# Two experts' slots filled at a time, 22 leading weight pieces, and narrower gathers in a streaming mixture-of-experts step

## The chip, the cores and the metric

The kernel runs on one core of a Trainium2 chip. The metric is the device time of one execution in microseconds (us): here the median of three runs. The program's engines are PE (TensorE), DVE (VectorE), ACT (ScalarE), POOL (GpSimd) and SP (SyncE, which here only issues loads). The core's 16 DMA engines are shared by all queues.

## What is computed

One layer of a hybrid encoder for 256 prompt rows and 32 sample rows (288 rows, 2048 wide): a combined input projection, stick-breaking attention, a gated linear recurrence, two gated projections and an output projection. Then a mixture of experts, which is the part that the change touches:

```python
def hmoe(h, wg, bg, ws, bs, wu, wd):
    hf = h.reshape(-1, d)
    g_logits = (hf @ wg) + bg
    _, g_idx = lax.top_k(g_logits, 1)                 # one of 4 groups
    ...
    e_val, e_idx = lax.top_k(sub_sel, TOP_K)          # two of its 4 experts
    e_w = jax.nn.softmax(e_val, axis=-1) * p_g
    combine = jnp.sum(one_hot(g_idx * 4 + e_idx, 16) * e_w[..., None], axis=1)
    for e in range(N_EXPERTS):                        # 16
        gate, up = jnp.split(hf @ wu[e], 2, axis=-1)  # wu[e]: 2048 x 1024
        out = out + combine[:, e:e+1] * ((silu(gate) * up) @ wd[e])   # wd[e]: 512 x 2048
```

Inputs and weights are float32. After it comes a final RMSNorm with a gain.

## The kernel before

**The stages.** Projections and attention run first and fill about 1080 us; their weights pass through four `ring` buffers. The output projection (`wo`, 16 column tiles) follows, with the router's logits. The experts come last.

**The experts' weights.** They are a stream of 192 pieces of 1 MB each (`STREAM`): 12 of each expert, 8 of `expert_w_up` ("up", two of the 16 row blocks k each) and 4 of `expert_w_down` ("down"). Pieces are numbered 0 to 191 here. Piece n goes to buffer `SLOT[n]` of `raw`. 16 buffers are permanent (`PERM`), and `ONCE = 4` more are used once, so `LEAD = 20` pieces can be loaded before any has been used. SP issues the pieces in order, each behind a wait: pieces 0 to 16 behind the progress of `wo`; piece 17 behind the first gather (`xs_in`) and the writes that it reads (`x1_out`), since its buffer lies where the table and the rows of before were; and from piece 20 on piece n waits until PE has used up the piece that was in its buffer (`eh_done`). From there on SP is 16 pieces ahead of PE at most.

**The rows.** An expert works on up to 64 rows. Per group of four experts, POOL gathers the group's rows (up to `CAP = 96`) from a table in DRAM into `xs`, in one indirect DMA of 128 rows of 7,680 bytes and one of 512 bytes each. PE then multiplies the transposed rows by one-hot matrices `R` ("spread"), one product for each of the 16 row blocks k, 256 columns wide (4 experts of 64 slots); two of them fill a PSUM bank. ACT and DVE empty the banks into `hgs`, multiplied by the norm's gain. Expert 0 can use its first piece when the first blocks are in `hgs`.

**The order of work** of PE, ACT and DVE around the pieces is written out by hand in half pieces t (piece n is t = 2n and 2n + 1). Tables say at which t something is slipped in: `SPREAD_AT` the spreads, `FIRST_ROWS` and `ROWS_AT` the transposes of `R` into `RT` and `es`, `META_AT` the next group's slots, `RESIDUAL_AT` four products that put the residual rows `xs` into the output banks `out4` (after which POOL may gather the next group into `xs`), `ADD_AT` the products that add an expert's output. `DOWN_AT[e]` is the t of expert e's first down piece; `DOWN_AT[0]` is 20 and `DOWN_AT[1]` is 44. `keep_warm(count)` issues that many products whose result nobody reads, while PE has nothing else to do.

Of the kernel before, what the change touches and what calls it, by code (L numbers as in the profile page):

```python
# [14 lines left out]
F32 = mybir.dt.float32  # L15
# [7 lines left out]
P = 128  # L23
# [27 lines left out]
PERM, ONCE = 16, 4  # L51
# [23 lines left out]
SLOT = [*range(13), *range(PERM, LEAD), *range(13, PERM)] + [n % PERM for n in range(PIECES - LEAD)]  # L75
# [43 lines left out]
NCONST, NCONST2 = 21, 13  # L119

# [33 lines left out]
def build(nc, x_prompt, x_sample, cache_k, cache_v, state_conv, state_lru, norm1_g, w_in, conv_w,  # L154
# [128 lines left out]
    lgT = sb("lgT", [40, T])  # L283
    best = sb("best", [TB, 5, 5 * FT, 4])
# [7 lines left out]
    hgs = sb("hgs", [P, 2, KT, EPG, ES])  # L292
    at_hgs1 = here[0] - 2 * 8192
# [33 lines left out]
    xs = sb("xs", [P, D])  # L327
    at_yo = here[0]
    yo = sb("yo", [CAP, D])
    gain = sb("gain", [P, D])  # L330
# [4 lines left out]
    here[0] = at_hgs1  # L335
    raw += [sb(f"raw{s}", [P, 2048]) for s in range(PERM + 2, LEAD)]
    assert here[0] <= at_o
    here[0] = at_prow
# [22 lines left out]
    up_v = expert_w_up[0].rearrange("e (p k) n -> p e k n", k=KT)  # L361
# [11 lines left out]
    with ExitStack() as ctx:  # L373
# [10 lines left out]
        trio = [bank[0:2], bank[2:4], bank[4:6]]  # L384

        x_in = [sem(f"x_in{f}") for f in range(FT)]
        par_in, rw_in, gain_in, gup_in = sem("par_in"), sem("rw_in"), sem("gain_in"), sem("gup_in")
# [58 lines left out]
        def spread_bank(q, c):  # L446

            return trio[q % 3][c] if q < SPREAD else work
# [15 lines left out]
        def _(sp):  # L464
# [12 lines left out]
            sp.dma_start(gup[:, :], norm2_g[0].rearrange("(p k) -> p k", k=KT)).then_inc(gup_in, 16)  # L477
# [53 lines left out]
            for dst, src in ((wr[:, :, 0:4], router_group_w[0].rearrange("(k p) g -> p k g", p=P)),  # L531
# [4 lines left out]
                sp.dma_start(dst, src).then_inc(rw_in, 16)  # L536
            gated_loads(T_PA, COL["ga"], w_pa_v)

            def fetch(slot, e, s, by_half=False):

                dst = raw[slot][:, :]
                if s < PU:
                    src = up_v[:, e, 2 * s:2 * s + 2, :]
                    dst = dst.rearrange("p (a k n) -> p a k n", a=1, k=2)
# [19 lines left out]
            for n, (e, s) in enumerate(STREAM):  # L564
# [6 lines left out]
                elif n == 14:  # L571
                    sp.wait_ge(half_done, 2 * T_END)
                elif n == 17:
                    sp.wait_ge(x1_out, 16 * len(X1_PARTS) + 16)
                    sp.wait_ge(token_ps, 2)
                    sp.wait_ge(xs_in, 16)
                elif n >= LEAD:
                    sp.wait_ge(eh_done, 2 * BEFORE[n] + 2)
                fetch(SLOT[n], ds(e, 1), s, e == NE - 1)
                if n == GAIN_AT:  # L580
                    sp.wait_ge(eh_done, 2 * SLOT.index(GAIN_SLOT) + 2)
                    sp.dma_start(gain[:, :], final_norm_g.rearrange("(a n) -> a n", a=1).partition_broadcast(P))\
# [23 lines left out]
        def _(pool):  # L606
# [98 lines left out]
            for g in range(NG):  # L705
                if g + 1 < NG:
                    pool.wait_ge(token_ready, g + 2)
                    pool.wait_ge(outB, SPREAD * (g + 1))
# [20 lines left out]
        def _(a):  # L729
# [247 lines left out]

            def drain_spread(q):

                a.wait_ge(spreadA_ps, q + 1)  # L980
                for c in range(2):
                    k = 4 * (q % SPREAD) + c
                    ins = a.activation(hgs[:, q // SPREAD % 2, k, :, :].rearrange("p e s -> p (e s)"),
                                       spread_bank(q, 0)[:, 256 * c:256 * (c + 1)], ACT.Copy, scale=gup[:, k:k + 1])
# [58 lines left out]
            a.wait_ge(gup_in, 16)  # L1043
            for q in range(2):
                drain_spread(q)
            for t in range(HALF_N):
# [16 lines left out]
                if t == FIRST_ROWS:  # L1063
                    rows(0, bank[2])
# [3 lines left out]
                for q, at in enumerate(SPREAD_AT):  # L1068
                    if t == at[0]:
# [14 lines left out]
            with a.If(n > CAP):  # L1084
                def again(v, first, width):

                    with a.Fori(0, NG) as g:
                        with a.Fori(0, width) as w:
# [5 lines left out]
                            for k in range(KT):  # L1094
                                a.wait_ge(ovhg_ps, KT * it + k + 1)
                                a.activation(hgs[:, 0, k, :, :].rearrange("p e s -> p (e s)"),
                                             bank[4 + k % 4][:, 0:EPG * ES], ACT.Copy, scale=gup[:, k:k + 1])\
# [29 lines left out]
        def _(pe):  # L1127
            pe.wait_ge(consts2, NCONST2)
            pe.wait_ge(par_in, 16 * 9)
# [289 lines left out]
            def spread(dst, k):  # L1419

                return pe.matmul(dst.rearrange("p (e s) -> p e s", e=EPG), xs[0:CAP, k::KT], R[:, :, 0, :].bitcast(F32),
# [713 lines left out]
```

## Time and profile before

| | us |
|---|---|
| median of three runs (1686.56 to 1687.59) | 1687.1 |
| the profiled execution's own time | 1686.14 |
| its span, first to last instruction | 1684.3 |
| PE busy in it | 1610.3 |
| DVE busy | 720.2 |
| ACT busy | 639.7 |
| POOL busy | 139.1 |

The profile is of one execution. Its times count from the first instruction; 1.8 us of the execution's own time lie outside of the span. Matmuls are pipelined, so that a row with several of them ends later than the next begins; the start of the next row says more. A DMA's "us to landing" is from the issue to the last part's completion.

### The profile page before, as it was taken

Reading aid. Unit: us, or ns where it says so; the run is one execution under the profiler, and the core shown is the slowest. Engines: PE = TensorE matmul, PEld = TensorE weight load, DVE = VectorE, ACT = ScalarE, POOL = GpSimd, SP = SyncE. Lnnn points to the kernel's source line nnn. Section 1 sums busy time; section 2 is a strip of 40 time slices with the busy share of each in tenths; the row PEclk is TensorE's granted clock in tenths of the full one; section 3 lists DMA queues with packets and bytes.
Section 4 is the critical chain, followed back from the end, with each engine's and each line's share of the span. In section 5 each row is a group of like instructions: output and inputs, shape, how many; then the busy total and the mean of one; then the engine's idle time right before and its main releaser. Section 6 shows DMA issues by size and latency. Waiting matters only on the chain. (4 is left out here: it accounts for less than half of the span.)

```text
span 1684.3 us, 27482 instructions
## 1 busy us (share of the span) xinstructions
PE 1610.3 (96%) x10714; PEld 1295.7 (77%) x10714; DVE 720.2 (43%) x1072; ACT 639.7 (38%) x1078; POOL 139.1 (8%) x189
## 2 busy tenths in 40 slices
PE   5999999999999999999999999999999999989885
PEld 4999999999999999999999999999734334323221
DVE  5888886443445455455454444544310201101101
ACT  6666665333344444444443333544211211111202
POOL 1644441000000000000000000000000000000000
PEclk9999999999999999999999999999999999999998
DMA  8465556566656546546478567795899999999995
GB/s 215 129 165 159 152 160 177 150 172 177 189 145 190 146 139 189 151 133 187 86 202 217 150 168 188 207 298 180 301 359 422 421 421 421 421 421 421 422 421 233
DMA packets 404519, 400.28 MB, mean 238 GB/s; under 512 B 19504, under 2 KB 377248, under 8 KB 379392
## 3 DMA queue, kind: packets, MB, share of 16 engines
q1 hardware_dynamic: 391456, 383.31, 69.2%
q0 software_dynamic: 2560, 11.21, 2.1%
q10 hardware_dynamic: 10432, 4.79, 1.1%
q8 instruction: 47, 0.77, 0.2%
q14 instruction: 24, 0.20, 0.0%
HBM read 389.77 MB, written 13.43 MB: 239 GB/s over the span
## 5 line engine op out<-in xcount | busy, mean ns | idle before, releaser
L1164 PE MATMUL bank<-hH,wH 128*128 128x288 f32 x1792 | 536.1, 299 | 6.2 <-ACTq L799 2.7
L1615 DVE TENSOR_TENSOR wL<-ring,wH 128x1024 fp32r<-128x1024 f32 x320 | 387.9, 1230 | 353.7 <-ACT wH L736 346.1
L736 ACT ACTIVATE wH<-ring 128x1024 fp32r<-128x1024 f32 x320 | 335.6, 1058 | 517.3 <-PE bank L1166 446.8
L1165 PE MATMUL bank<-hL,wH 128*128 128x288 f32 x1792 | 528.9, 295 | 0.0
L1166 PE MATMUL bank<-hH,wL 128*128 128x288 f32 x1792 | 528.5, 295 | 0.0
L1164 PEld LDWEIGHTS bank<-hH,wH 128*128 128x128 f32 x1792 | 337.3, 188 | 13.5 <-issue 7.0
L1165 PEld LDWEIGHTS bank<-hL,wH 128*128 128x128 f32 x1792 | 337.4, 188 | 0.3
L1166 PEld LDWEIGHTS bank<-hH,wL 128*128 128x128 f32 x1792 | 337.2, 188 | 0.0
L1396 PE MATMUL bank<-raw,hgs 128*64 128x512 f32 x1024 | 242.7, 600 | 18.9 <-DMA raw<-in_expert_w_up 15.3
L1396 PEld LDWEIGHTS bank<-raw,hgs 128*64 128x64 f32 x1024 | 66.6, 136 | 162.2 <-issue 110.5
L1164 PE MATMUL bank<-oH,wH 128*128 128x288 f32 x512 | 150.7, 294 | 0.5 <-DVE oL L1712 0.5
L1165 PE MATMUL bank<-oL,wH 128*128 128x288 f32 x512 | 151.0, 295 | 0.0
L1166 PE MATMUL bank<-oH,wL 128*128 128x288 f32 x512 | 150.9, 295 | 0.0
L1396 PE MATMUL bank<-raw,actT 128*64 128x512 f32 x512 | 124.7, 601 | 8.3 <-DMA raw<-in_expert_w_down 7.8
L1984 DVE SCALAR_TENSOR_TENSOR silu<-bank,es,silu 64x512 f32<-64x512 f32 x16 | 12.1, 757 | 265.7 <-ACT silu L1020 265.7
L1164 PEld LDWEIGHTS bank<-oH,wH 128*128 128x128 f32 x512 | 96.3, 188 | 1.0 <-DVE oL L1712 0.7
L1165 PEld LDWEIGHTS bank<-oL,wH 128*128 128x128 f32 x512 | 96.3, 188 | 0.0
L1166 PEld LDWEIGHTS bank<-oH,wL 128*128 128x128 f32 x512 | 96.2, 188 | 0.0
L1396 PEld LDWEIGHTS bank<-raw,actT 128*64 128x64 f32 x512 | 32.9, 136 | 78.3 <-issue 56.8
L1020 ACT ACTIVATE silu<-bank,es 64x512 f32<-64x512 f32 x16 | 10.9, 681 | 198.7 <-PE bank L1396 198.6
L1350 PE MATMUL bank<-hH,wH 128*128 128x288 f32 x256 | 76.4, 299 | 0.0
L1351 PE MATMUL bank<-hL,wH 128*128 128x288 f32 x256 | 75.5, 295 | 0.0
(312 smaller groups left out, 1538.4 us busy)
## 6 DMA issues: line engine op xcount, KB each, us to landing
raw<-in_expert_w_up SPq DMA_DIRECT2D x128, 1024.0 KB, 26.0
ring<-in_w_in SPq DMA_DIRECT2D x112, 1024.0 KB, 6.3
raw<-in_expert_w_down SPq DMA_DIRECT2D x64, 1024.0 KB, 26.5
ring<-in_w_pb SPq DMA_DIRECT2D x16, 1024.0 KB, 9.1
ring<-in_w_pa SPq DMA_DIRECT2D x16, 1024.0 KB, 9.1
ring<-in_w_o SPq DMA_DIRECT2D x16, 1024.0 KB, 6.1
cK<-in_cache_k SPq DMA_DIRECT2D x16, 256.0 KB, 2.8
cV<-in_cache_v SPq DMA_DIRECT2D x16, 256.0 KB, 3.2
```

The source lines that it names most:

```text
L736: a.activation(wH[2 * (slot % 2) + half][:, :, :], ring[slot][:, 8 * half:8 * half + 8, :], ACT.Copy).then_inc(hi_ready, 1)
L1020: a.activation(silu[ES:P, :], upb[0:ES, :], ACT.Silu, scale=es[0:ES, e // EPG % 2, e % EPG, 4:5]).then_inc(silu_ready, 1)
L1164: pe.matmul(dst, hi, rH[:, k, :], start=(k == 0), stop=False)
L1165: pe.matmul(dst, hi, rL[:, k, :], start=False, stop=False)
L1166: ins = pe.matmul(dst, lo, rH[:, k, :], start=False, stop=(k == KT - 1))
L1350: pe.matmul(dst, hi, hH[:, k, :], start=(k == 0), stop=False, skip_group_check=True)
L1351: pe.matmul(dst, hi, hL[:, k, :], start=False, stop=False, skip_group_check=True)
L1396: ins = pe.matmul(dst[c * ES:(c + 1) * ES, :], w, raw[slot][:, 1024 * half + 512 * c:1024 * half + 512 * (c + 1)], start=first, stop=last)
L1615: v.tensor_tensor(lo[:, :, :], ring[slot][:, 8 * half:8 * half + 8, :], hi[:, :, :].bitcast(F32), ALU.subtract).then_inc(lo_ready, 1)
L1984: v.scalar_tensor_tensor(silu[ES:P, :], upb[ES:P, :], es[ES:P, e // EPG % 2, e % EPG, e % EPG:e % EPG + 1], silu[ES:P, :], ALU.mult, ALU.m ...
```

## The change

The numbering of pieces and of t stays, the order of `STREAM` too. What differs:

- **Two experts at a time.** `hgs` is laid out by group, pair of experts, k. For group 0 the spread is done for experts 0 and 1 first (products of 128 columns, four to a bank, `pair_step`, two banks ahead of the first piece and one each ahead of pieces 2 and 4), and for experts 2 and 3 between the halves of pieces 15 to 18. The other groups keep products of 256 columns. DVE empties the first bank of a step and ACT the second.
- **22 leading pieces.** `ONCE` is 6. The buffers used once lie partly in the space of `hgs`' other pairs. Piece 13 now waits for the end of `wo` (it did not). Pieces 14 to 17 follow without a wait, piece 18 behind the logits (`lg_ps`), and it is piece 19 that waits for the gather. From piece 22 on a piece waits for `eh_done`.
- **Later group work.** `ASSIGN_AT`, `META_AT`, `ROWS_AT` and `RESIDUAL_AT` count from the group's second expert, 24 half pieces later (the residual 18 later). The residual products no longer start the banks: expert 0's `add_rows` does.
- **96-row transfers.** The gathers and the final gain's broadcast fill 96 partitions in place of 128.
- **Layout of the up weights.** The 2048 input rows are assigned to partitions in blocks of 256 (two neighbouring rows a partition), so an up piece is 1 MB in one run of DRAM, where it was 128 runs of 8 KB, 64 KB apart. `gup` follows, in runs of 8 bytes (1,024) where it was 64 bytes (128), and its landing is among those that PE's first instruction waits for. The rows' columns are now read two apart for a product's weights, where it was 16 apart.
- `keep_warm(6)` after the first group's token product becomes `keep_warm(14)`.

```diff
-PERM, ONCE = 16, 4
+PERM, ONCE = 16, 6
-SLOT = [*range(13), *range(PERM, LEAD), *range(13, PERM)] + [n % PERM for n in range(PIECES - LEAD)]
+SLOT = [*range(13), PERM + 2, PERM, PERM + 1, *range(PERM + 3, LEAD), *range(13, PERM)] + [n % PERM for n in range(PIECES - LEAD)]
...
-ASSIGN_AT = [DOWN_AT[EPG * g] for g in range(NG - 1)]
-META_AT = [DOWN_AT[EPG * g] + 2 for g in range(NG - 1)]
-ROWS_AT = [DOWN_AT[EPG * g] + 6 for g in range(NG - 1)]
-RESIDUAL_AT = [DOWN_AT[EPG * g] + 10 for g in range(NG)]
-FIRST_ROWS = 8
-SPREAD_AT = [(None, None)] * 2 + [(2, 2), (4, 4)]
+ASSIGN_AT = [DOWN_AT[EPG * g + 1] for g in range(NG - 1)]
+META_AT = [DOWN_AT[EPG * g + 1] + 2 for g in range(NG - 1)]
+ROWS_AT = [DOWN_AT[EPG * g + 1] + 6 for g in range(NG - 1)]
+RESIDUAL_AT = [DOWN_AT[EPG * g + 1] + 4 for g in range(NG)]
+FIRST_ROWS = 12
+SPREAD_AT = [(None, None), (4, 8)] + [(DOWN_AT[0] + 11 + 4 * r, DOWN_AT[0] + 13 + 4 * r) for r in range(2)]
...
-    up_v = expert_w_up[0].rearrange("e (p k) n -> p e k n", k=KT)
+    up_v = expert_w_up[0].rearrange("e (s p k) n -> p e s k n", p=P, k=2)
...
-            sp.dma_start(gup[:, :], norm2_g[0].rearrange("(p k) -> p k", k=KT)).then_inc(gup_in, 16)
+            sp.dma_start(gup[:, :].rearrange("p (s k) -> p s k", k=2),
+                         norm2_g[0].rearrange("(s p k) -> p s k", p=P, k=2)).then_inc(par_in, 16)
...
-                elif n == 14:
+                elif n == 13:
                     sp.wait_ge(half_done, 2 * T_END)
-                elif n == 17:
+                elif n == 18:
+                    sp.wait_ge(lg_ps, 1)
+                elif n == 19:
                     sp.wait_ge(x1_out, 16 * len(X1_PARTS) + 16)
                     sp.wait_ge(token_ps, 2)
                     sp.wait_ge(xs_in, 16)
...
-                                            bass.IndirectOffsetOnAxis(ap=idx[:, column, 2:3], axis=0),
+                                            bass.IndirectOffsetOnAxis(ap=idx[0:CAP, column, 2:3], axis=0),
...
-                return pe.matmul(dst.rearrange("p (e s) -> p e s", e=EPG), xs[0:CAP, k::KT], R[:, :, 0, :].bitcast(F32),
+                c = 2 * P * (k // 2) + k % 2
+                return pe.matmul(dst.rearrange("p (e s) -> p e s", e=count), xs[:, c:c + 2 * P - 1:2],
+                                 R[:, first:first + count, 0, :].bitcast(F32),
                                  start=True, stop=True, skip_group_check=True)
...
-            keep_warm(6)
+            keep_warm(14)
...
-            for q in range(2):
-                spread_step(q, 0)
-                spread_step(q, 1)
+            pair_step(0, 0)
+            pair_step(0, 1)
```

**PE from the wait for the gather to piece 4.** `hH` rows are keep-warm products, `R,xs` rows spreads, `raw,hgs` rows up pieces (four products each), `ident,R` rows the transposes into `RT`. Before:

```order
L1320 MATMUL bank<-hH 128x288 x20
L1421 MATMUL bank<-R,xs 128x256 [waits R_ready,xs_in,last_ready]
L1421 MATMUL bank<-R,xs 128x256 x7
L1396 MATMUL bank<-raw_136,hgs 64x512 [waits raw_in0,outA,routed]
L1396 MATMUL bank<-raw_136,hgs 64x512 x3
L1421 MATMUL bank<-R,xs 128x256 [waits outB]
L1421 MATMUL bank<-R,xs 128x256 x3
L1396 MATMUL bank<-raw_137,hgs 64x512 [waits raw_in1]
L1396 MATMUL bank<-raw_137,hgs 64x512 x3
L1421 MATMUL bank<-R,xs 128x256 [waits outA]
```

After:

```order
L1337 MATMUL bank<-hH 128x288 x20
L1439 MATMUL bank<-R,xs 128x128 [waits R_ready,xs_in]
L1439 MATMUL bank<-R,xs 128x128 x7
L1413 MATMUL bank<-raw_136,hgs 64x512 [waits raw_in0,outB,routed]
L1413 MATMUL bank<-raw_136,hgs 64x512 x3
L1413 MATMUL bank<-raw_137,hgs 64x512 [waits raw_in1,outB]
L1413 MATMUL bank<-raw_137,hgs 64x512 x3
L1439 MATMUL bank<-R,xs 128x128 [waits outA]
L1439 MATMUL bank<-R,xs 128x128 x3
L1413 MATMUL bank<-raw_138,hgs 64x512 [waits raw_in2]
```

The eight spreads ahead of piece 0 are half as wide and cover all that pieces 0 to 3 need.

**SP from piece 12 to the piece behind the gather and the first ones behind `eh_done`.** Before (pieces 12 to 20):

```order
L552 DMA raw_183<-in_expert_w_up 128x2048 [waits half_done]
L552 DMA raw_187<-in_expert_w_down 128x2048
L552 DMA raw_188<-in_expert_w_up 128x2048 [waits half_done]
L552 DMA raw_189<-in_expert_w_up 128x2048
L552 DMA raw_190<-in_expert_w_down 128x2048
L552 DMA raw_160<-in_expert_w_up 128x2048 [waits xs_in,token_ps,x1_out]
L552 DMA raw_161<-in_expert_w_up 128x2048
L552 DMA raw_162<-in_expert_w_down 128x2048
L552 DMA raw_136<-in_expert_w_up 128x2048 [waits eh_done]
```

After (pieces 12 to 22):

```order
L556 DMA raw_183<-in_expert_w_up 128x2048 [waits half_done]
L556 DMA raw_189<-in_expert_w_down 128x2048 [waits half_done]
L556 DMA raw_187<-in_expert_w_up 128x2048
L556 DMA raw_188<-in_expert_w_up 128x2048
L556 DMA raw_190<-in_expert_w_down 128x2048
L556 DMA raw_191<-in_expert_w_up 128x2048
L556 DMA raw_192<-in_expert_w_up 128x2048 [waits lg_ps]
L556 DMA raw_160<-in_expert_w_down 128x2048 [waits xs_in,token_ps,x1_out]
L556 DMA raw_161<-in_expert_w_up 128x2048
L556 DMA raw_162<-in_expert_w_up 128x2048
L556 DMA raw_136<-in_expert_w_down 128x2048 [waits eh_done]
```

Piece 13 has moved behind the end of `wo`, and two more pieces stand ahead of the wait for the gather.

## Rows read from the trace of the kernel before

**Rows 1.** Page, part 2: the span in 40 slices of 42 us.

```profile
DMA  8465556566656546546478567795899999999995
GB/s 215 129 165 159 152 160 177 150 172 177 189 145 190 146 139 189 151 133 187 86 202 217 150 168 188 207 298 180 301 359 422 421 421 421 421 421 421 422 421 233
```

**Rows 2.** Stretches: length, engines' busy time (rows), PE clock, DMA share, GB/s.

```profile
1199.00:1204.00 5.00, 4.27 (x23) 4.27 (x24) 2.05 (x14) 0.00 (x0) 0.88 (x2) 0.66 0.71 226
1207.00:1214.00 7.00, 7.00 (x31) 3.86 (x29) 1.74 (x3) 1.68 (x4) 0.00 (x0) 1.00 1.01 427
1248.00:1256.00 8.00, 8.00 (x37) 2.64 (x38) 0.00 (x0) 0.50 (x1) 2.09 (x2) 1.00 0.58 183
1262.00:1600.00 338.00, 319.39 (x1432) 114.78 (x1430) 47.16 (x91) 56.73 (x109) 9.71 (x10) 1.00 1.01 421
```

**Rows 3.** Timeline of SP's queue: start, length with waits between, issues.

```profile
1187.76 1.07 SPq L552 DMA_DIRECT2D raw<-in_expert_w_up  x2
1188.88 0.66 SPq L552 DMA_DIRECT2D raw<-in_expert_w_down  x1
1204.57 0.80 SPq L552 DMA_DIRECT2D raw<-in_expert_w_up  x2
...
1239.91 14.12 SPq L552 DMA_DIRECT2D raw<-in_expert_w_up  x2
1255.41 0.33 SPq L552 DMA_DIRECT2D raw<-in_expert_w_down  x1
```

**Rows 4.** Timeline of PE, 1199 to 1249 us: start, length, instructions, idle before.

```profile
1199.73 0.68 PE L1405 MATMUL bank<-meta,G 96*96 96x12 f32 x6 [1.32 <-DVEq L1948]
1200.26 4.43 PE L1320 MATMUL bank<-hH 128*128 128x288 f32 x20
1204.53 3.81 PE L1421 MATMUL bank<-R,xs 96*128 96x256 f32 x16
1208.27 1.94 PE L1396 MATMUL bank<-raw,hgs 128*64 128x512 f32 x8
1210.14 2.15 PE L1421 MATMUL bank<-R,xs 96*128 96x256 f32 x8
1212.21 1.94 PE L1396 MATMUL bank<-raw,hgs 128*64 128x512 f32 x8
...
1219.74 0.55 PE L1411 MATMUL bank<-ident,R 96*128 96x96 f32 x4
1220.13 0.98 PE L1415 MATMUL bank<-ms,R 96*128 96x5 f32 x8
1221.04 7.09 PE L1396 MATMUL bank<-raw,hgs 128*64 128x512 f32 x32
1229.76 1.94 PE L1396 MATMUL bank<-raw,hgs 128*64 128x512 f32 x8 [1.63 <-DVE silu L1984]
...
1244.68 3.67 PE L1446 MATMUL bank<-xs,ident 96*96 96x512 f32 x8
1248.28 1.94 PE L1396 MATMUL bank<-raw,hgs 128*64 128x512 f32 x8
```

**Rows 5.** DMA issues at 1198, 1358, 1253.7 and 1255.4 us: us to landing.

```profile
xs<-x_rows,idx POOLq DMA_INDIRECT x1, 6.1
...
xs<-x_rows,idx POOLq DMA_INDIRECT x1, 10.0
...
raw<-in_expert_w_up SPq DMA_DIRECT2D x1, 1024.0 KB, 4.9
...
raw<-in_expert_w_down SPq DMA_DIRECT2D x1, 1024.0 KB, 7.2
```

**Rows 6.** Groups by line and shape, 1190 to 1262 us: busy us, mean ns.

```profile
L1421 PE MATMUL bank<-R,xs 96*128 96x256 f32 x32 | 8.1, 401 | 0.0
...
L1421 PEld LDWEIGHTS bank<-R,xs 96*128 96x128 f32 x32 | 7.3, 307 | 1.6 <-issue 1.6
...
L1481 PE MATMUL bank<-x,G 96*96 96x128 f32 x6 | 0.9, 282 | 0.0
```

**Rows 7.** The keep-warm line alone, 1200.6 to 1204.0 us: PE, PEld, PE clock.

```profile
1200.60:1204.00 3.40, 3.40 (x17) 3.40 (x16) 0.50 0.74 287
```

**Rows 8.** A stretch of 16-byte packets; ACT's first weight tile at the start.

```profile
836.00:841.00 5.00, 5.00 (x37) 3.85 (x36) 2.91 (x3) 2.19 (x6) 0.00 (x0) 1.00 0.89 26
19.16 2.00 ACT L736 ACTIVATE wH<-ring 128x1024 fp32r<-128x1024 f32 x2 [1.90 <-DMA ring<-in_w_in]
```

More of the change, by code:

```diff
@@ L334, in build @@
     assert here[0] <= at_prow
-    here[0] = at_hgs1
-    raw += [sb(f"raw{s}", [P, 2048]) for s in range(PERM + 2, LEAD)]
+    here[0] = at_hgs + 8192
+    raw += [sb(f"raw{s}", [P, 2048]) for s in range(PERM + 2, PERM + 5)]
     assert here[0] <= at_o
+    here[0] = at_prow
+    raw += [sb(f"raw{s}", [P, 2048]) for s in range(PERM + 5, LEAD)]
     here[0] = at_prow
@@ L976, in _, with drain_pair @@
             a.activation(xs[0:CAP, LAST:], bank[5][0:CAP, 0:P], ACT.Copy).then_inc(last_ready, 1)
+            def drain_pair(q):
+                a.wait_ge(spreadA_ps, q + 1)
+                for c in range(4):
+                    k = 8 * (q % 2) + 4 + c
+                    ins = a.activation(hgs[:, 0, q // 2, k, :, :].rearrange("p e s -> p (e s)"),
+                                       spread_bank(q, 1)[:, P * c:P * (c + 1)], ACT.Copy, scale=gup[:, k:k + 1])
+                ins.then_inc(outA, 1)
             def drain_spread(q):
@@ L1063, in _ @@
                 if t == FIRST_ROWS:
-                    rows(0, bank[2])
+                    rows(0, bank[4])
                 for g in range(NG - 1):
@@ L1417, in row_turn, with spread, pair_step @@
                 ins.then_inc(rows_ps, 1)
-            def spread(dst, k):
-                return pe.matmul(dst.rearrange("p (e s) -> p e s", e=EPG), xs[0:CAP, k::KT], R[:, :, 0, :].bitcast(F32),
+            def spread(dst, k, first=0, count=EPG):
+                c = 2 * P * (k // 2) + k % 2
+                return pe.matmul(dst.rearrange("p (e s) -> p e s", e=count), xs[:, c:c + 2 * P - 1:2],
+                                 R[:, first:first + count, 0, :].bitcast(F32),
                                  start=True, stop=True, skip_group_check=True)
+            def pair_step(q, c):
+                if q >= 2 and c == 0:
+                    need(pe, outA, q if q > 2 else 0)
+                elif q >= 2:
+                    pe.wait_ge(outB, q + 1)
+                if q == 0 and c == 0:
+                    pe.wait_ge(xs_in, 16)
+                    pe.wait_ge(R_ready, 1)
+                if q == 1 and c == 1:
+                    pe.wait_ge(last_ready, 1)
+                dst = spread_bank(q, c)
+                for kk in range(4):
+                    ins = spread(dst[:, P * kk:P * (kk + 1)], 8 * (q % 2) + 4 * c + kk, 2 * (q // 2), 2)
+                ins.then_inc((spreadB_ps, spreadA_ps)[c], 1)
             def spread_step(q, c):
                 n, r = q // SPREAD, q % SPREAD
-                if n == 0:
-                    need(pe, (outA, outB)[c], q - 2)
-                elif c == 0:
+                if c == 0:
                     pe.wait_ge(outB, q)
@@ L1437, in spread_step, with residual @@
                     pe.wait_ge(R_ready, n + 1)
-                dst = spread_bank(q, c)
                 for kk in range(2):
-                    ins = spread(dst[:, 256 * kk:256 * (kk + 1)], 4 * r + 2 * c + kk)
+                    ins = spread(work[:, 256 * kk:256 * (kk + 1)], 4 * r + 2 * c + kk)
                 ins.then_inc((spreadA_ps, spreadB_ps)[c], 1)
-            def residual():
+            def residual(first):
                 for nb in range(4):
-                    ins = pe.matmul(out4[nb][0:CAP, :], ident[0:CAP, 0:CAP], xs[0:CAP, nb * 512:(nb + 1) * 512],
-                                    start=True, stop=False, skip_group_check=True)
+                    ins = pe.matmul(out4[nb][0:CAP, :], ident[0:CAP, 0:CAP], xs[:, nb * 512:(nb + 1) * 512],
+                                    start=first, stop=False, skip_group_check=True)
                 return ins
@@ L1454, in act_turn, with add_rows @@
                 ins.then_inc(at_ps, 1)
-            def add_rows(buf, j, last):
+            def add_rows(buf, j, last, first=False):
                 for half in range(2):
@@ L1462, in add_rows @@
                             ins = pe.matmul(out4[2 * half + c][0:CAP, :], RT[rows, buf, j, :], y[rows, half, :],
-                                            start=False, stop=last and y is yL, skip_group_check=True)
+                                            start=first and y is yH, stop=last and y is yL, skip_group_check=True)
                     ins.then_inc(sum_ps, 1)
@@ L1860, in _ @@
             v.wait_ge(logit_ps, KT)
-            own.step(v.memset(idx[CAP:P, :, 2:3], 0))
             v.tensor_copy(lgT[:, :], bank[4][0:40, 0:T]).then_inc(lgT_ready, 1)
@@ L2023, in _ @@
             v.tensor_copy(cnt_i[:, :], cmax[:, :]).then_inc(routed, 1)
-            v.wait_ge(gup_in, 16)
-            for q in range(2):
-                drain_spread(q)
+            v.wait_ge(par_in, 16 * NPARAM)
+            drain_pair(0)
             for t in range(HALF_N):
@@ L2041, in _ @@
                 if t == FIRST_ROWS:
-                    columns(bank[2], 0, 0)
+                    columns(bank[4], 0, 0)
                 for g in range(NG - 1):
```

103 lines of the change are left out of this document (60 added, 43 removed).

## The prediction

> **What bounds the kernel now.** I read the page's slices first [rows 1]: from slice 30 on (about 1,260 us) the 16 DMA engines are full at 421 GB/s to the end; before that their share goes up and down between 2 and 9 tenths, while PE is busy. So there are two regimes: PE paces the projections, the transfers pace the experts. The stretches say it more finely [rows 2]: 1,262 to 1,600 us moves 421 GB/s, so a piece of 1.049 MB costs 2.49 us there, and whatever moves the moment at which that stream becomes continuous, or the bytes in it, moves the end one for one. What follows the last piece (the last products, norm, scatter) isn't touched.
>
> The part between is where the change acts: 1,199 to 1,204 us moves 226 GB/s, and 1,248 to 1,256 us moves 183 GB/s [rows 2]. SP's queue says what ends each hole [rows 3]. The first: piece 16 is issued by 1,189.5, piece 17 at 1,204.57, behind the gather. The second: pieces 32 and 33 are one row from 1,239.91 of 14.12 us, so that piece 33 is issued at 1,253.7, when PE had used up piece 17, and it lands 4.9 us later [rows 5]. The second hole counts: it shows that until 1,253.7 PE's progress and not the first hole sets the stream. PE's clock for it starts at T = 1,204.53, the first spread [rows 4]. Piece 33 is issued at T + 49.2 and landed at T + 54.1.
>
> **PE's work from T, step by step.** From the starts in [rows 4]: the first spreads take 3.74 (1,204.53 to 1,208.27), 16 matmuls of 256 columns at 0.222 and 0.2 of change-over. A piece is 1.72 (four in 7.09, the last one's tail off). A later spread block is 2.07, with its change-over 2.2. The transposes into `RT` are 1.3 (1,219.74 to 1,221.04), 1.4 with theirs. The stall for `silu` behind piece 7 is 1.63, about 1.8. The residual is 3.60 (1,244.68 to 1,248.28), 3.7. I take 0.75 for the slots' product (its first use took 0.68 [rows 4]) and 0.5 for expert 0's small transposes, an estimate from the 0.55 of four others there.
>
> - Before, up to the use of piece 17: 3.7 + 2 x 2.2 + 2 x 1.4 + 1.8 + 0.75 + 0.5 + 3.7 + 18 x 1.72 = 48.6; measured 49.2, so 0.6 is missing from my list.
> - After, piece 35 waits for piece 19, the last but one of the three behind the gather's wait. In between stand six blocks of four narrow spreads. A narrow product, 128 columns wide, isn't in the trace with these operands. The nearest row is L1481, 128 columns with 96 rows: six in 0.9, starts 0.11 apart [rows 6], half of the 0.222. The upper bound is 0.222, if not the columns but the load of the weights sets the pace (307 ns each for the spreads, overlapped [rows 6]); the lower bound is 0.11. I take 0.11, since all matmuls of that width run at it. So 16 x 0.11 + 0.2 = 2.0 ahead of piece 0 and 8 x 0.11 + 0.4 = 1.3 for each of the six blocks. Slots, second transposes and residual come behind piece 21. Sum: 2.0 + 7.8 + 1.4 + 1.8 + 0.5 + 20 x 1.72 + 0.6 = 48.5.
>
> So piece 35 lands at T + 48.5 + 4.9 = T + 53.4, where piece 33 did at T + 54.1: two pieces further, 0.7 earlier. **2 x 2.49 + 0.7 = 5.7 us gained**, against T. The earlier pieces don't limit: 22 to 34 follow each other at 2.49 from about 1,217, the last at about 1,250.
>
> **What is given back.** The gather of group 1 ran in the old hole (1,248 to 1,256 at 183 GB/s). It moves behind the residual at piece 24, into the full stream: 96 x 8,192 bytes = 0.79 MB, at 421 GB/s **+1.9 us**. The residual itself (3.7) stands between pieces 23 and 24, so pieces 40 and on are issued later; gain vector and gather, 1.9 us each, are moved in that time, so I cost it at nothing; without that cover it would be 2.7.
>
> **Bytes.** 32 rows of 8 KB less: 0.26 MB or 0.62 us in the gathers of groups 2 and 3 and in the gain's broadcast, all in the full stream: **-1.9 us**. The up weights' new layout: 8 KB packets as before; up and down pieces, which already lie in one run, share one rate in the full stretch, so nothing. The spread outputs' layout costs ACT and DVE nothing that PE waits for: a bank is emptied in 0.7 to 1 us under a piece of 1.72.
>
> **T moves.** Before, the first gather had the DMA engines to itself: it was issued at 1,198.0 and landed 6.1 us later; one beside a full queue took 10.0 [rows 5]. Now six pieces (13 to 18, 15 us of transfer) are issued from 1,187.7 to 1,191, and their data is under way until about 1,206. With a quarter of its bytes less the gather takes some 8.8 instead of 10.0 (4.6 of those 10.0 are its data at half the rate, an estimate from 983 KB at 211 GB/s, half of 421), 2.7 more than 6.1. Before, PE began 0.4 behind the landing, since keep-warm products were in its way; now it begins at once: T is about **+2.3 us** later. Bounds: 0, if the gather still takes 6.1, and +3.9. The Trainium skill (DMA: Bandwidth & Descriptors, "Queues, rings and completion order") says that a DMA engine goes round the rows of queues packet by packet; the 10.0 agrees with it. The same page's fit for such a DMA ("Anatomy of one DMA", 2.0 us + bytes / 436 GB/s) gives 3.7 us for the new gather, by which T wouldn't move; for the old one it gives 4.3, and the row has 6.1, so the row decides.
>
> **The clock.** Before, 1.32 us of idle time ahead of the slots' product was followed by a stretch at a granted 0.50, 1.2 GHz, in which 17 keep-warm products took 3.4 us [rows 4, 7]; they filled just the time until the gather. With `keep_warm(14)` the idle time is filled, the 20 that follow need 20 x 0.14 = 2.9 at 2.4 GHz and end near 1,203.1. Then PE has nothing until 1,206.8: 3.7 us idle, more than what cost it the clock before. I expect the low clock over the first spreads and pieces. A stretch like the one above, 3.4 us at half, costs **+1.7 us**. Bounds: 0 and 3.4.
>
> **The start.** `gup` is 1,024 packets of 8 bytes ahead of the first weight tiles, 896 more. The router's 16-byte packets moved at 26 GB/s, 1.6 a ns [rows 8], so that is 0.55 us. ACT waits for that tile at 19.16 [rows 8] and PE behind it: **+0.5 us**, bounds 0 and 1. The wait for `gup` at PE's first instruction is covered by ACT, which waits for the tile anyway. Piece 13's delay costs nothing, as six pieces now queue up behind the end of `wo` in any case.
>
> **Sum**, against the profiled execution's 1,686.14: -5.7 + 1.9 - 1.9 + 2.3 + 1.7 + 0.5 = -1.2, so 1,684.9. The median of the runs is 1.0 above that execution: **1,685.9**.
>
> **Rivals.**
> - *The gather isn't late and PE's clock stays high.* For it: the gather's first data came slowly even with all engines free (226 GB/s over the stretch with it [rows 2]), so half of the engines may be enough. Against it: 10.0 under load. Then 2.3 and 1.7 fall away: 1,681.9. If only the clock stays high, 1,684.2.
> - *Slower: narrow spreads cost what wide ones do.* If the weights' load sets 0.22 a matmul, 64 of them cost 64 x 0.11 = 7.0 more ahead of piece 19: 1,692.9. It decides from about 0.18 a matmul, where the 4.6 us that separate the forecast from slower by 0.2% are used up. For it: the load of 307 ns is the longest of PE's in this stretch. Against it: with a step of 16 columns it was hidden under 0.222, and the step is 2 now.
> - *The change does nothing to the end.* If the stream after piece 35 has new holes (pieces 36 to 40 are issued each just in time, and piece 34 took 7.2 to land in such a place [rows 5]), the gain is eaten up, 2 to 3 us more: about 1,688.
> - A per-core limit near 358 GB/s for DRAM, which the Trainium skill states (DMA: Bandwidth & Descriptors, Specifications), would make a piece 2.93 us; the stretch at 421 says no, and nothing above uses it.
>
> **Chances.** The forecast as worked 0.42; gather and clock both undisturbed 0.28; the clock alone 0.08; new holes 0.10; dear spreads 0.12. ±0.2% (3.4 us) is about what a measurement of this kernel tells from no change. Faster by more, below 1,683.7: the second case and a few of the forecast's, 0.33. Slower by more, above 1,690.5: the dear spreads and a bit of the others, 0.14. The same: 0.53. The forecast's own range is 1,683 to 1,688 (gather and clock to half their bounds). 8 in 10 need the undisturbed case too, with 1 us below it for a shorter stall at piece 36, and upwards part of the way to dear spreads: 1,680.8 to 1,690.0.
>
> **What the profile after would show.** SP: seven issues between 1,188 and 1,191 and the next behind the gather, near 1,207. PE: spreads in 2.0 (3.6 if cold) near 1,207 with idle time ahead of them and a clock of 0.50 in the row. Piece 35 issued at the first spread + 48.5. The full stream from about 1,262, and the last piece's use some 1 us earlier than before. The prediction is wrong if the gather lands before 1,205, if narrow spreads start more than 0.15 apart, or if the stream has holes behind piece 36.

## The result, and the profile after

The changed kernel takes 1699.77 us (median of 4 runs, 1699.47 to 1701.06), the kernel before 1686.83 us (4 runs beside it, 1686.49 to 1687.59). The ratio is 1.0078 with a 95% interval of 1.006 to 1.0095. The forecast was 1685.9, in a range of 1680.8 to 1690.0. The change makes the kernel slower by 13 us.

The page of the changed kernel, part 2, in 40 slices of 42 us, answers to [rows 1].

```profile
DMA  9466556566656546645577666784979999999995
GB/s 212 114 167 163 153 161 177 149 175 171 188 145 186 160 137 173 172 134 161 112 200 191 177 169 176 227 294 163 352 313 378 422 401 422 421 399 421 422 421 221
```

The DMA engines are full from slice 30 on, as before, but the rate isn't: 378, 401 and 399 GB/s in slices 30, 32 and 35, where every slice had 421 or 422. Those are the places of the gathers. Stretches of the changed kernel show it (columns as in [rows 2]); the second is the hole ahead of piece 35, which answers to 1,248 to 1,256 before.

```profile
1262.00:1600.00 338.00, 315.49 (x1432) 108.36 (x1430) 48.63 (x101) 54.82 (x108) 11.64 (x12) 1.00 1.01 407
...
1254.00:1261.00 7.00, 7.00 (x38) 3.29 (x36) 0.89 (x2) 2.08 (x7) 0.00 (x0) 1.00 0.02 8
...
1268.00:1290.00 22.00, 22.00 (x102) 7.99 (x98) 2.04 (x9) 1.74 (x3) 2.00 (x2) 1.00 1.00 321
1384.00:1396.00 12.00, 12.00 (x64) 4.84 (x65) 0.18 (x1) 0.70 (x2) 0.98 (x1) 1.00 1.01 351
1504.00:1516.00 12.00, 9.16 (x42) 2.73 (x41) 0.18 (x1) 0.49 (x1) 0.18 (x1) 1.00 1.02 342
1294.00:1380.00 86.00, 84.78 (x392) 30.30 (x391) 14.25 (x30) 16.45 (x32) 1.92 (x2) 1.00 1.01 421
```

Between the gathers the stream has its old 421 GB/s (1,294 to 1,380). Beside the gain vector and the gather of group 1 (1,268 to 1,290) it has 321, beside the gathers of groups 2 and 3 351 and 342, with a DMA share of 1.00 to 1.02: the engines are occupied, but move less. A full share is no proof of full rate.

The beginning of the expert stage, first in SP's queue, then on PE (columns as in [rows 3] and [rows 4]; the issues are now line 556, the warming products 1337, the slots' product 1422, spreads 1439, pieces 1413).

```profile
1190.46 1.39 SPq L556 DMA_DIRECT2D raw<-in_expert_w_up  x2
1191.90 0.76 SPq L556 DMA_DIRECT2D raw<-in_expert_w_down  x1
1192.70 1.00 SPq L556 DMA_DIRECT2D raw<-in_expert_w_up  x2
1212.30 0.33 SPq L556 DMA_DIRECT2D raw<-in_expert_w_down  x1
...
1244.47 0.33 SPq L556 DMA_DIRECT2D raw<-in_expert_w_down  x1
1261.64 2.27 SPq L556 DMA_DIRECT2D raw<-in_expert_w_up  x2
```

```profile
1201.90 0.68 PE L1422 MATMUL bank<-meta,G 96*96 96x12 f32 x6 [0.22 <-DVEq L1982]
1202.43 2.91 PE L1337 MATMUL bank<-hH 128*128 128x288 f32 x20
1211.05 3.78 PE L1439 MATMUL bank<-R,xs 96*128 96x128 f32 x16 [5.70 <-DMA xs<-x_rows,idx]
1214.76 4.36 PE L1413 MATMUL bank<-raw,hgs 128*64 128x512 f32 x16
1219.05 1.21 PE L1439 MATMUL bank<-R,xs 96*128 96x128 f32 x8
```

The first gather, issued at 1,200.25, takes 10.8 us instead of 6.1 (the row of issues, columns as in [rows 5]):

```profile
xs<-x_rows,idx POOLq DMA_INDIRECT x1, 10.8
```

PE is idle for 5.70 us before it, and then has the low clock until 1,216.2:

```profile
1202.43:1205.40 2.97, 2.91 (x22) 2.68 (x21) 1.52 (x9) 0.00 (x0) 0.00 (x0) 1.00 1.03 401
1209.40:1216.20 6.80, 5.15 (x20) 4.02 (x22) 0.69 (x1) 1.14 (x4) 0.00 (x0) 0.50 0.70 257
```

5.15 us of work at 0.50 would have been half as long at 1.00: the low clock costs 2.6 us. A block of narrow spreads takes 1.21 us once the clock is up. Its eight products start 0.12 us apart, near the 0.11 forecast, so narrow spreads are cheap.

**One difference is only partly the change's.** The changed execution is 2.3 us late already at a tile of `wo`: SP issues it at 1,085.92 instead of 1,083.60. The first product starts when it did (23.10 us, 23.09 before). Later in the start PE had a stretch at half clock. The same stretch of four kernels, 44 to 60 us (columns as in [rows 2]): before, changed, the kernel before with 96-row gathers, and the changed one with three pieces ahead and full transfers (the last two are experiments below).

```profile
44.00:60.00 16.00, 14.20 (x104) 13.75 (x104) 12.74 (x18) 9.07 (x13) 13.43 (x14) 1.00 0.37 102
```

```profile
44.00:60.00 16.00, 14.20 (x92) 13.64 (x92) 12.82 (x17) 9.03 (x13) 14.34 (x15) 0.89 0.30 79
```

```profile
44.00:60.00 16.00, 14.20 (x93) 13.56 (x92) 12.68 (x19) 8.54 (x12) 13.84 (x15) 0.89 0.32 86
```

```profile
44.00:60.00 16.00, 14.20 (x104) 13.75 (x104) 12.78 (x19) 9.73 (x14) 14.09 (x15) 1.00 0.33 90
```

The third kernel has the start of the kernel before, word for word, and shows 0.89; the fourth has the start of the changed one and shows 1.00. So the dip occurs with either start: in one of five executions with the old start and in six of nine with the new one, over all kernels below. It doesn't explain all of the lateness. Without the dip the `wo` tile is issued at 1,083.0 to 1,083.7 with the old start (four executions) and at 1,084.4 to 1,085.4 with the new one (three); with the dip at 1,085.4 (one) and 1,085.1 to 1,086.1 (six). Nearly all of it is there by 75 us. Some 1 to 2 us may thus be the change's own; no experiment separates them. To compare profiled executions without this lateness I use the **way**: the time from the issue of that `wo` tile to the landing of the last piece. It is 582.8 us before (1,083.6 to 1,666.4) and 595.5 changed (1,085.9 to 1,681.4): +12.7 us, near the 12.9 of the medians. A way is that of one execution, and leaves out whatever the change costs in the start. It is good to about 1.5 us: within the full stream a piece sometimes lands 0.9 to 1.5 us late where nothing of the change is at work (between pieces 177 and 178 in four of the kernels below), each time beside a packet of 16,384 bytes of the queue that loads instructions, though most such packets pass without it. The changed execution's own last piece is such a case: its last packet ends 3.4 us after the piece before has landed, in the others 2.0 to 2.1.

### The profile page after: what moved, and what is told of

Same layout as the page of the kernel before. It is cut to its first block and busy times, and to the rows that moved or that the text cites. A ratio compares the mean times of both kernels' runs of the same rounds, so it can differ in the third digit from the quotient of the medians.

```text
span 1698.1 us, 27573 instructions
## 1 busy us (share of the span) xinstructions
PE 1614.8 (95%) x10754; PEld 1293.1 (76%) x10754; DVE 720.3 (42%) x1071; ACT 641.0 (38%) x1086; POOL 138.7 (8%) x189
## 5 line engine op out<-in xcount | busy, mean ns | idle before, releaser
L1183 PE MATMUL bank<-hH,wL 128*128 128x288 f32 x1792 | 529.3, 295 | 0.0
L1413 PE MATMUL bank<-raw,actT 128*64 128x512 f32 x512 | 125.0, 602 | 10.7 <-DMA raw<-in_expert_w_down 10.2
L1413 PEld LDWEIGHTS bank<-raw,actT 128*64 128x64 f32 x512 | 32.4, 136 | 82.0 <-issue 53.6
L1369 PE MATMUL bank<-hH,wL 128*128 128x288 f32 x256 | 75.3, 294 | 0.0
```

The costliest lines, as they stand in the source:

```text
L1183: ins = pe.matmul(dst, lo, rH[:, k, :], start=False, stop=(k == KT - 1))
L1369: ins = pe.matmul(dst, lo, hH[:, k, :], start=False, stop=False, skip_group_check=True)
L1413: ins = pe.matmul(dst[c * ES:(c + 1) * ES, :], w, raw[slot][:, 1024 * half + 512 * c:1024 * half + 512 * (c + 1)], start=first, stop=last)
```

## The experiments

All stand against the kernel before, run on the same chip beside them: 1686.8 us in the median for the changed kernel, 1688.2 to 1688.7 for the others. They ran in three groups, each on a chip of its own, so rows of different groups are compared by their ratios. "Way" is the one above.

| kernel | median us | ratio [95%] | way, against before's |
|---|---|---|---|
| changed | 1699.8 | 1.0078 [1.006, 1.0095] | +12.7 |
| changed, gain 128 wide | 1698.3 | 1.0051 [1.0038, 1.0065] | +9.0 |
| changed, gathers 128 wide | 1693.8 | 1.0037 [1.0025, 1.005] | +5.7 |
| changed, both 128 wide | 1692.5 | 1.0025 [1.0015, 1.0036] | +4.1 |
| the same, unused rows skipped | 1691.7 | 1.002 [1.001, 1.0029] | +5.4 |
| both 128 wide, 54 warming products | 1690.2 | 1.0011 [1.0002, 1.002] | +2.3 |
| both 128 wide, three pieces ahead | 1685.6 | 0.9988 [0.9979, 0.9997] | -1.3 |
| the same, skipped rows, 30 warming | 1685.3 | 0.9983 [0.9974, 0.9992] | -1.9 |
| changed, three pieces ahead | 1692.4 | 1.0017 [1.0008, 1.0026] | +4.4 |
| before, gathers and gain 96 wide | 1693.1 | 1.0031 [1.0021, 1.0041] | +4.9 |
| before, gathers and gain 112 wide | 1694.9 | 1.0034 [1.0021, 1.0046] | +5.2 |
| before, gain in two halves of 64 | 1691.9 | 1.002 [1.0011, 1.003] | +3.6 |
| before, unused rows skipped | 1687.2 | 0.9999 [0.999, 1.0008] | -0.5 |

The first theory, N: a transfer into 96 partitions moves slowly and holds back the weights beside it, so that "32 rows less" costs time. The rival, L: the late first gather, the cold start of PE and the new order cost it all. Four kernels told them apart.

**Gathers 128 rows wide again** (the gain stays at 96).

```diff
-xs = sb("xs", [CAP, D])
+xs = sb("xs", [P, D])
-bass.IndirectOffsetOnAxis(ap=idx[0:CAP, column, 2:3], axis=0)
+bass.IndirectOffsetOnAxis(ap=idx[:, column, 2:3], axis=0)
+own.step(v.memset(idx[CAP:P, :, 2:3], 0))
```

> The changed kernel with its gathers 128 rows wide again (128 partitions of the rows tile), all else as changed, the gain's broadcast 96 wide too. Theory N (transfers that fill 96 partitions move slowly and hold back the weight pieces beside them): the gathers of groups 1 to 3 give back about 3 us each, so about 1,690 to 1,693 us. Rival L (the loss is PE's late and cold start and the new order of its work): about 1,700 to 1,701, as only bytes come back.

**Gathers and gain 128 wide**: the same, and

```diff
-gain = sb("gain", [CAP, D])  ... partition_broadcast(CAP)
+gain = sb("gain", [P, D])    ... partition_broadcast(P)
```

> The changed kernel with both the gathers and the gain's broadcast 128 partitions wide. Theory N: of the 12 us that the stretch behind piece 35 took over the forecast, about 10 go away: 1,688 to 1,690 us, and the GB/s beside each gather is again 420. Rival L: 1,700 to 1,702.

**The kernel before with gathers and gain at 96** (the same edits the other way round).

> The kernel before with only the gathers and the gain's broadcast cut to 96 partitions. Theory N: slower, by 3 to 3.5 us for each of the gathers of groups 2 and 3, 3 for the gain, something for that of group 1 in its hole: 1,695 to 1,699 us. Rival L, and the forecast's term for bytes: 1.9 us faster than before, about 1,685.

**128 wide, with the last 32 indices out of bounds**, so that their rows aren't moved: `memset(idx[CAP:P, :, 2:3], 4096)` instead of 0, gain 128 wide.

> The changed kernel with gathers that are 128 partitions wide but whose last 32 indices lie out of bounds, so that these rows are skipped and 96 rows are moved; gain 128 wide. Theory N in the form that the spread of the rows over partitions and engines counts: as fast as with 128 rows or up to 1.5 us faster, 1,686.5 to 1,690 us. If instead the number of moved rows (96) makes it slow: 1,696 to 1,700.

Measured: 1.0037, 1.0025, 1.0031 and 1.002. All four lie on N's side; in microseconds all four miss N's ranges, by 0.8 to 2.5 us (1693.8, 1692.5, 1693.1 and 1691.7). Width alone takes two thirds of the loss from the changed kernel (from +12.7 to +4.1 us of way) and gives the kernel before a loss that it didn't have (+4.9). L alone is ruled out, and so is "fewer rows are slow": with only 96 rows moved, but through a 128-wide transfer, the kernel is by its runs as fast as with 128 rows (its one profiled way is 1.3 us longer; there the low clock behind the gather lasted longer, so that the first pieces took 5.67 us instead of 4.45). The stretches of the changed kernel with both 128 wide, against 321, 351 and 342 above:

```profile
1268.00:1290.00 22.00, 22.00 (x101) 8.03 (x102) 2.94 (x11) 2.37 (x4) 2.09 (x2) 1.00 1.01 416
1384.00:1396.00 12.00, 12.00 (x58) 4.05 (x58) 0.68 (x2) 1.55 (x3) 0.26 (x1) 1.00 1.02 419
1504.00:1516.00 12.00, 9.63 (x46) 2.68 (x44) 2.14 (x3) 1.93 (x4) 0.00 (x0) 1.00 1.01 420
```

There remained 0.25%. **54 instead of 20 warming products** ahead of the first spread, both 128 wide:

```diff
-keep_warm(20)
+keep_warm(54)
```

> The version with 128-row gathers and gain (1.0025 of before, 4.1 us over it), with 54 instead of 20 warming matmuls ahead of the first spread: TensorE then works until about the time the first gather lands. If the rest of the loss is the cold clock behind the wait (0.50 for some 7 us, priced 2.6 us), piece 35 lands some 2.5 us earlier, the span is about 1687.5 and the ratio about 1.001. If the rest is only the gather's own lateness, or the weight stream hides the clock, it stays at 1.0025.

Its PE, and the stretch behind the gather, first with 20 products, then with 54:

```profile
1209.95 3.78 PE L1439 MATMUL bank<-R,xs 96*128 96x128 f32 x16 [4.93 <-DMA xs<-x_rows,idx]
```

```profile
1209.60:1216.40 6.80, 6.45 (x26) 4.45 (x28) 0.69 (x1) 1.14 (x4) 0.00 (x0) 0.58 0.60 221
```

```profile
1201.85 7.45 PE L1337 MATMUL bank<-hH 128*128 128x288 f32 x54
1209.65 2.15 PE L1439 MATMUL bank<-R,xs 96*128 96x128 f32 x16 [0.36 <-DMA xs<-x_rows,idx]
```

```profile
1209.60:1216.40 6.80, 6.75 (x40) 4.24 (x40) 0.69 (x1) 1.14 (x4) 0.00 (x0) 1.00 0.63 230
```

The clock is 1.00 where it was 0.58, the 16 first spreads take 2.15 instead of 3.78, piece 35 is issued at T + 48.3 instead of T + 50.7, the way is 1.8 us shorter and the ratio 1.0011. The rows show the low clock's share at about 2 us, some half of the 4.1 us of way that are left with six pieces ahead; the ratios alone, 1.0025 and 1.0011 with intervals that overlap, wouldn't.

**Three pieces ahead of the first gather**, as before, instead of six (both 128 wide, 20 warming products):

```diff
+elif n == 16:
+    sp.wait_ge(x1_out, 16 * len(X1_PARTS) + 16)
+    sp.wait_ge(xs_in, 16)
 elif n == 18:
     sp.wait_ge(lg_ps, 1)
 elif n == 19:
-    sp.wait_ge(x1_out, 16 * len(X1_PARTS) + 16)
     sp.wait_ge(token_ps, 2)
-    sp.wait_ge(xs_in, 16)
```

> The same version, with SyncE's wait for the first gather at piece 16 instead of 19: three pieces (13 to 15) ahead of the gather as before, instead of six. If the lateness of the gather is the rest of the loss, the gather lands about 4 us earlier (6 us from its issue instead of 10), TensorE has no idle time of 5 us and no cold clock, piece 35 lands 4 to 6 us earlier, and the ratio is 0.998 to 1.000. If what is gained there is paid back by pieces 16 to 18 that come late for TensorE, the first spread is earlier but piece 35 is not, and the ratio stays at 1.0025.

It is the first kernel that beats the one before, by 0.1%: 0.9988. Its issue of the gather, PE and SP:

```profile
xs<-x_rows,idx POOLq DMA_INDIRECT x1, 6.1
```

```profile
1201.03 2.90 PE L1338 MATMUL bank<-hH 128*128 128x288 f32 x20
1204.97 2.15 PE L1440 MATMUL bank<-R,xs 96*128 96x128 f32 x16 [1.03 <-DMA xs<-x_rows,idx]
```

```profile
1236.09 0.33 SPq L556 DMA_DIRECT2D raw<-in_expert_w_down  x1
1253.27 2.27 SPq L556 DMA_DIRECT2D raw<-in_expert_w_up  x2
```

The gather takes 6.1 us again, T is 1,204.97, there is no cold stretch, and piece 35 is issued at T + 48.3. The three pieces that now come behind the gather cost PE nothing: piece 19, issued after them, lands at 1,217.7, and PE is done with it at 1,253.2, as far behind T as forecast.

**The kernel before with its unused rows skipped** (one edit, `memset(idx[CAP:P, :, 2:3], 4096)`).

> The kernel before, whose gathers stay 128 rows wide, with the 32 unused indices out of bounds so that their rows are not moved (they are row 0 otherwise). If what costs is the spread over 96 partitions and not the bytes, the gathers of groups 2 and 3 cost about 0.6 us less each: ratio 0.999 (1.3 us less, and at most 2 with the first two gathers). If moving 96 rows is slow in itself, as in the kernel before with 96-row gathers, it is 1.003.

The ratio is 0.9999 [0.999, 1.0008], no difference; the one way is 0.5 us shorter. I expected 1.3 us for two gathers. The interval doesn't exclude that, so it is shown only that the bytes of the 32 rows are worth little beside the 4.9 us that 96 partitions cost.

**All of it in the changed kernel**: 128 wide, skipped rows, three pieces ahead, 30 warming products.

> All that the runs point to, in the changed kernel: gathers 128 wide that skip the 32 unused rows, gain 128 wide, three pieces ahead of the first gather, 30 warming matmuls. If the parts add up, 0.8 us less than the version with three ahead: ratio 0.997 to 0.999, that is faster than before by the 4 to 6 us that the new order was forecast to bring, less 2.4 for the gather of group 1 that no longer lies in a hole. If the new order has no worth of its own, 1.000 or above.

0.9983, which can't be told from the 0.9988 of the version without skipping and warming. Both are faster than the kernel before.

Four more asked what it is about 96 partitions, and whether the causes add up.

**The changed kernel with the gain alone at 128.**

> The changed kernel with the gain loaded into 128 partitions again and its gathers left at 96 rows. With gathers and gain both at 128 the ratio went from 1.0078 to 1.0025, with the gathers alone to 1.0037. If every 96-partition transfer inside the weight stream costs about the same in its bytes (0.75 MB each, four of them), the gain alone brings about a quarter, 2 us: ratio 1.0065. If the gain costs nothing by itself it stays at 1.0078.

It brings 3.7 us of way, 1.0051: more than the quarter that I expected. The gathers alone brought 7.0, both together 8.6, less than the sum of 10.7. That isn't shown to be an overlap in the stretch from 1,268 to 1,290, where the two lie side by side: at piece 42, just behind it, the gain has brought 1.9, the gathers 2.3 and both 4.0. The rest comes later and is of the size of the ways' scatter.

**The kernel before with the gain in two transfers of 64 partitions**, the same bytes:

```diff
-sp.dma_start(gain[:, :], ...partition_broadcast(P)).then_inc(gain_in, 16)
+for h in range(2):
+    sp.dma_start(gain[64 * h:64 * h + 64, :], ...partition_broadcast(64)).then_inc(gain_in, 16)
-v.wait_ge(gain_in, 16)
+v.wait_ge(gain_in, 32)
```

> The kernel before, with the gain loaded in two transfers of 64 partitions each instead of one of 128; same bytes. If a transfer is slow because its rows are dealt to the 16 engines otherwise than those of a 128-partition transfer (4 a piece instead of 8), the packets of gain and of the weights beside it take well over 320 ns on the mean, the stretch moves 250 to 350 GB/s and the kernel is 1 to 2.5 us longer: ratio 1.0005 to 1.0015. If only an unfilled last quarter is what costs, nothing changes: 1.000 and packets at 310 to 320 ns.

Slower by 0.2%, 3.6 us of way, more than the 2.5 us that I expected at most; all of it is there at piece 40, behind the gain. The same nine microseconds, first of the kernel before, then with the halves:

```profile
1266.00:1275.00 9.00, 9.00 (x44) 3.02 (x42) 0.00 (x0) 0.00 (x0) 0.00 (x0) 1.00 1.01 425
```

```profile
1266.00:1275.00 9.00, 9.00 (x44) 3.02 (x42) 0.00 (x0) 0.00 (x0) 0.00 (x0) 1.00 1.00 255
```

**The kernel before with gathers and gain over 112 partitions** (xs, gain, the indices and the broadcast cut to 112).

> The kernel before with gathers and gain over 112 partitions instead of 128 (7 rows for each of the 16 engines). If it is the dealing out of rows otherwise than by 8 that costs, it is about as slow as with 96 partitions (1.0031): 1.002 to 1.004. If the cost grows with the partitions that are left out, it is half of that, 1.0015. If 112 are as good as 128, 1.000 and packets of the gathers at 295 ns.

As slow as with 96 (1.0034 against 1.0031), though only an eighth is left out instead of a quarter. The stretch of group 2's gather, 1,362 to 1,371 us, of the kernel before and of this one:

```profile
1362.00:1371.00 9.00, 7.78 (x40) 2.32 (x36) 2.04 (x3) 3.43 (x5) 0.00 (x0) 1.00 1.01 418
```

```profile
1362.00:1371.00 9.00, 7.78 (x40) 2.43 (x36) 2.04 (x3) 3.43 (x5) 0.00 (x0) 1.00 1.02 313
```

**The changed kernel with three pieces ahead, transfers at 96.**

> The changed kernel as it is (gathers and gain at 96), with only the wait for the first gather moved to piece 16, so that three pieces are ahead of it. With 128-partition transfers this brought 6.2 us (1.0025 to 0.9988). If the two causes are independent it brings the same here: ratio 1.004. If the lateness of the gather comes from its 96 rows as well, it brings more, up to 1.003; if the 96-partition transfers then take back what is gained, less, 1.006.

1.0017, better than the 1.004 expected. By the ways the two causes aren't quite independent: width costs 8.6 us with six pieces ahead (+12.7 against +4.1) and 5.7 with three (+4.4 against -1.3). Why it costs more with six isn't settled. Of the 2.9 us between the two, 1.4 are the late last piece of the changed execution, and 0.8 lie ahead of T: with six pieces ahead the first gather lands 10.8 us after its issue at 96 rows and 10.0 at 128, with three 6.0 and 6.1.

The packets of the traces tell the same, counted by size between 1,262 and 1,600 us; 8,192 bytes are those of weights and gain, 7,680 those of the gathers:

| kernel | 8,192 bytes: mean ns | of them over 400 ns | 7,680 bytes: mean ns | GB/s |
|---|---|---|---|---|
| before | 313.8 | 19 | 294 | 421 |
| before, 112 wide | 318.2 | 394 | 431 | 413 |
| before, 96 wide | 319.2 | 418 | 433 | 412 |
| before, gain in halves | 317.8 | 213 | 294 | 416 |
| changed | 321.2 | 548 | 427 | 407 |
| changed, both 128 wide | 314.5 | 46 | 297 | 419 |
| changed, skipped rows | 315.1 | 68 | 298 | 418 |

## Why the prediction was wrong

**The step that failed is "Bytes", -1.9 us.** It took 96-row transfers as 128-row ones with a quarter less of data. The runs give it the other sign: between the changed kernel and the same with full width lie 8.6 us of way (1.0078 against 1.0025), where the forecast had 1.9 the other way. The transfers lost more than their own quarter: a packet of a gather takes 427 ns instead of 294, and hundreds of packets of the weights beside them over 400 instead of 310. The forecast's +1.9 for the gather that leaves its hole has the same fault. In the hole, where the queue was empty, the slow packets cost little: in the old order group 1's gather lands 5.6 us after its issue at 96 rows and 5.2 at 128. Within the stream they hold back a queue that sets the end. The same width costs 8.6 us in the changed kernel and 4.9 in the old order, which fits with that; it wasn't tried by itself. The mechanism was in no rival. Nor would a sign of being wrong that the prediction named have shown it: the gather landed after 1,205, narrow spreads started 0.12 apart and there was no hole behind piece 36. But there was a hint: at the very start of the kernel before, where hardly anything but rows of x is loaded, in transfers of 96, 64 and 32 partitions, the engines are busy at 0.98 and move 219 GB/s, while [rows 2] has 421 at nearly the same share. A packet of 8,192 bytes takes 584 ns there, and 314 in the full stream.

```profile
2.00:11.00 9.00, 0.00 (x0) 0.00 (x0) 0.00 (x0) 3.79 (x4) 3.09 (x28) 1.00 0.98 219
```

What about the width costs is narrowed, not shown to the end. It isn't the bytes (skipping rows brings 0.5 us or nothing), nor how much of the last quarter is filled (112 are as slow as 96), nor what kind of transfer (the gain is a plain load, the gathers are indirect), nor a total that leaves partitions out: two halves of 64 with the whole bytes are slow too. What is left of my own candidates is how the rows are dealt to the 16 engines and where these write.

The Trainium skill has something near it. In its page DMA: Bandwidth & Descriptors, "The descriptor swizzle", each engine of a 128-partition transfer writes one port of the on-chip memory of its own. In SBUF — State Buffer, "Door 1: The DMA port swizzle", partitions 0 to 63 lie on eight of the 16 ports and 64 to 127 on the others, and bandwidth depends on how many ports the partitions reach. The halves agree with that, 255 GB/s against 425. For 96 and 112 partitions, which reach all 16 ports, it foretells no loss as it stands. By its map of ports 96 rows put 8 rows on each of eight ports and 4 on each of the others, so the fullest ports would save nothing. That engines then share a port and stand in each other's way, and so slow the packets beside them, is my inference from there. No trace here names the port of a packet, so it stays a guess.

**"T moves", +2.3, was of the right kind and too small.** The gather took 10.8 us and not 8.8. With 128 rows and the same six pieces ahead it took 10.0, just the 10.0 of [rows 5], so a quarter less of rows made it longer: the fault of "Bytes" again. T is 1,211.05 instead of 1,204.53, 6.5 later; counted from the `wo` tile, and so without the 2.3 of the start, it is 4.2, beyond the bound of +3.9.

**"The clock", +1.7, was right in kind, and 0.9 too small.** PE was idle for 5.70 us, longer than the 3.7 forecast, and the low clock cost 2.6 us by the row, 1.8 us of way when the longer warming took it away. Gather and clock together were put at 4.0; undoing both brings 5.4 us of way (+4.1 to -1.3).

**The work from T up to piece 19, 48.5, was right.** With three pieces ahead, piece 35 is issued at T + 48.3 and lands 5.3 us later, T + 53.6 (forecast T + 53.4). In the changed kernel it is issued at T + 50.6, since the low clock lies in between. The gain of the new order is real, and smaller than forecast. With everything else undone, 5.7 us should have been left less the gather that leaves its hole. That gather is 128 rows wide here, 1.05 MB, and costs 2.5 us at 421 GB/s, so 3.2 us. The kernel with three pieces ahead keeps 1.3 of way and 0.12% of time, 2.0 us. Part of what is missing can be placed: its stretch behind piece 35, with gain and group 1's gather, runs at 404 GB/s instead of 420, in 22 us 0.8 us less of transfer.

```profile
1262.00:1284.00 22.00, 22.00 (x102) 7.75 (x96) 2.58 (x6) 2.36 (x4) 2.09 (x2) 1.00 1.01 404
```

At piece 42, just behind that, the kernel is 2.1 us of way ahead of the one before, and still at piece 90. Another 0.9 goes at piece 101, beside a packet of instructions, and doesn't come back. Why the gather and the gain move at 404 even at full width stays open.

**The start, +0.5 for `gup`, isn't refuted.** In the two executions compared there is no difference: ACT's first weight tile comes at 19.17 instead of 19.16, PE's first product at 23.10 instead of 23.09. But executions differ by more than the term. The first product starts at 22.3 to 23.1 with the old start (five executions) and at 22.8 to 23.6 with the new one (nine), 0.46 later in the mean.

**The rivals.** Dear narrow spreads: no, 1.21 us a block. New holes behind piece 35: no hole once the stream is full (the share stays at 1.00), but a loss in that very place, larger and of another cause. The gather undisturbed: no, by the row of issues. The limit of 358 GB/s: no, 421 still stands between the gathers.

As a sum of ways: full width to 96 partitions +8.6, late gather and cold clock +5.4, the new order by itself -1.3: together the +12.7 that was measured. Against the forecast of -1.2 that is 13.9 more: 10.5 from the width (+8.6 where -1.9 stood), 1.4 from gather and clock (5.4 where 4.0 stood) and 2.0 from the new order with the start (-1.3 where -3.3 stood). These are ways of single executions; the medians, 0.53%, 0.37% and -0.12%, say the same within their intervals.

## What to carry to other kernels

A transfer into fewer than 128 partitions isn't a cheaper 128-partition transfer; that was measured for 96, 112 and 64. If it runs beside a stream that is bound by the DMA engines, fill it up to 128 partitions, with rows that nobody reads or indices that are skipped, and judge such a transfer by GB/s at full share, never by its bytes. Pieces issued ahead of a small transfer that an engine waits for delay it, here from 6.1 to 10.0 us with three pieces more; put ahead only what the engine needs before the small one, here three pieces and not six. An engine that must wait for longer than it did needs its warming lengthened with the wait.

## What the runs showed of the hardware that I had not expected

- 96, 112 and twice 64 partitions are all slow: packets of 7,680 bytes 427 to 433 ns instead of 294 at 96 and 112, and 213 (the halves) to 548 packets of 8,192 bytes over 400 ns, where there were 19.
- Rows that an index out of bounds skips brought no time that the runs can tell: 0.9999 [0.999, 1.0008], for 32 rows of 8 KB in each gather.
- PE's clock behind short idle times: 1.32 us idle was followed by a stretch at 0.50, 1.2 GHz [rows 4, 7], 5.70 us idle by one at 0.50 over the first 5 us of work, and 1.03 us (three pieces ahead) by first spreads at full speed, 2.15 us for 16.
- The clock's dip between 44 and 60 us comes with either kernel, and not in each execution. The one execution with the old start that has it issues the `wo` tile 1.8 us later than the kernel before, about as much as the best version gains.
